# RWKV-7 rounds of a hybrid diffusion backbone: another order, another substitution and another sharing of copies

## The reference, cut to what matters

```python
def rwkv7_scan(r, w, k, v, a, b, state):
    def step(S, inp):
        r_t, w_t, k_t, v_t, a_t, b_t = inp
        sa = jnp.einsum('bhvk,bhk->bhv', S, a_t)
        S = S * w_t[:, :, None, :] + sa[..., None] * b_t[:, :, None, :] + v_t[..., None] * k_t[:, :, None, :]
        return S, jnp.einsum('bhvk,bhk->bhv', S, r_t)
```

## Time and profile before

| what | us |
|---|---|
| median of three runs | 2333.25 (2330.16 to 2334.47) |
| span of the profiled execution, first to last instruction | 2316.3 |
| PE busy / PEld busy / DVE busy / ACT busy / POOL busy | 1964.1 / 1364.9 / 941.6 / 702.3 / 330.4 |
| the RWKV rounds (`rwkv_chunks`), from the first z product to the last addition to y | 1426.4 to 1846.8, 420.4 |
| of these: round 0 (front only), until the first X product | 20.6 |
| rounds 1 to 8 | 399.8 |

### The profile page before, as it was taken

How to read it: one execution, slowest core, us unless ns; L and a number is a source line. 1 busy time by engine, 2 the same in 40 slices (tenths; PEclk the granted TensorE clock), 3 DMA queues, 4 the chain that set the end, 5 groups by cost and what they waited for, 6 DMA issues and landing times. The chain is left out here.

```text
span 2316.3 us, 58391 instructions
## 1 busy us (share of the span) xinstructions
PE 1964.1 (85%) x26021; PEld 1364.9 (59%) x26021; DVE 941.6 (41%) x1675; ACT 702.3 (30%) x1525; POOL 330.4 (14%) x211
## 2 busy tenths in 40 slices
PE   6999998997979888998487895888888897977775
PEld 3777765445844445555253685888878755633443
DVE  3183235785051111111434577666777453111112
ACT  3234534674230000100214344455444212000001
POOL 1433310002401000000110345212311000000000
PEclk8999999998989989999799997999999977988888
DMA  8554533204265789777530220000000025899975
GB/s 298 189 204 146 183 144 146 74 1 145 73 258 217 280 302 349 277 272 285 212 111 1 70 77 28 4 5 5 4 4 4 31 91 206 301 387 365 358 295 182
DMA packets 133329, 381.14 MB, mean 165 GB/s; under 512 B 14394, under 2 KB 43670, under 8 KB 115926
## 3 DMA queue, kind: packets, MB, share of 16 engines
q1 hardware_dynamic: 114528, 343.82, 40.3%
q10 hardware_dynamic: 15094, 20.99, 3.0%
q0 software_dynamic: 3456, 12.58, 1.4%
HBM read 634.54 MB, written 25.95 MB: 285 GB/s over the span
## 5 line engine op out<-in xcount | busy, mean ns | idle before, releaser
L371 PE MATMUL banks<-parts 128*128 128x512 f32 (+1 forms) x1096 | 244.7, 375 | 14.5 <-POOL parts L1523 7.6
L1814 PE MATMUL banks<-arena 128*32 128x256 f32 x1696 | 218.4, 403 | 40.8 <-DMA arena<-in_exp_w_up_dram 40.8
L371 PEld LDWEIGHTS banks<-parts 128*128 128x128 f32 x1096 | 194.6, 192 | 55.2 <-POOL parts L2388 9.4
L1815 PE MATMUL banks<-arena 128*32 128x256 f32 x1696 | 218.3, 402 | 0.0
L2561 PE MATMUL banks<-arena 64*64 64x64 f32 x4224 | 159.4, 225 | 47.7 <-DVE arena L382 18.5
L1880 ACT ACTIVATE arena<-banks 64x256 f32<-64x256 f32 x78 | 29.6, 380 | 549.9 <-PE banks L1815 382.6
L2561 PEld LDWEIGHTS banks<-arena 64*64 64x64 f32 x4224 | 147.7, 140 | 52.3 <-DVE arena L382 19.9
L1814 PEld LDWEIGHTS banks<-arena 128*32 128x32 f32 x1696 | 102.0, 115 | 120.5 <-DMA arena<-in_exp_w_up_dram 44.0
L371 PE MATMUL banks<-arena,ring 128*128 128x256 f32 (+2 forms) x560 | 163.3, 459 | 9.4 <-PEq L318 8.5
L2561 PE MATMUL banks<-ring 64*64 64x64 f32 x4224 | 159.9, 225 | 8.6 <-issue 7.4
L379 DVE TENSOR_TENSOR arena<-banks,arena 64x256 f32<-64x256 f32 (+3 forms) x128 | 65.5, 511 | 241.5 <-ACT arena L1880 149.9
(11 more groups left out here) (373 smaller groups left out, 3626.8 us busy)
## 6 DMA issues: line engine op xcount, KB each, us to landing
arena<-in_exp_w_gate_dram SPq DMA_DIRECT2D x106, 1024.0 KB
arena<-in_exp_w_up_dram SPq DMA_DIRECT2D x106, 1024.0 KB
arena<-in_exp_w_down_dram SPq DMA_DIRECT2D x53, 2048.0 KB
ring<-in_exp_w_gate_dram SPq DMA_DIRECT2D x50, 1024.0 KB
ring<-in_exp_w_up_dram SPq DMA_DIRECT2D x50, 1024.0 KB
ring<-in_exp_w_down_dram SPq DMA_DIRECT2D x25, 2048.0 KB
ring<-in_w_mod_dram SPq DMA_DIRECT2D x24, 2048.0 KB, 8.9
ring<-in_ab_w_in_dram SPq DMA_DIRECT2D x10, 2048.0 KB, 13.9
```

The costliest lines, as they stand in the source:

```text
L371: m = nc.tensor.matmul(o, a, b, start=first and n == 0, stop=last and n == len(pairs) - 1)
L1814: nc.tensor.matmul(o[r:r + BLOCK, 0:256], x, up[:, k, c], start=k == 0, stop=k == KD - 1)
L1815: m = nc.tensor.matmul(o[64 + r:64 + r + BLOCK, 0:256], x, gate[:, k, c], start=k == 0, stop=k == KD - 1)
```

## The change

Layout and names: `natural` gets D4, D4t, K4t, T2, N, KN, Nt and V1, so that D4, D4t, T2, T4, D8t, N, Nt, N2, V1 and V2 run on all four tiles (`both`); D2, D2t, T8 and U remain on two (`each`). The wide products are gone; each result has a bank of its own.

Inverse: DVE (or ACT) no longer adds T2 and T4; instead K2t = D2t + 1 and K4t = D4t + 1 are formed from PSUM, and the products are T2 = K2t T1, T4 = K4t T2; only T8 is a sum with T4. Substitution: N, its transpose Nt (one more product), KN = N + 1 and N2 = Nt N; then V1 = T8 W, V2 = KN V1, U = N2 V2 + V2. Instead of three products in a row after V1 there are two, and N2 beside them.

Accumulation in PSUM: W is opened with AK vt and a S is added to it (`opening`, `adding`); Y is opened with S r and the two others are added to it. The wide product a (S b) is therefore split into a S and Xt.

Order: the products X and Xt of the next round (`pe first`, `pe second`), their masks and T1 on DVE (`dve first`, `second`, `third`), and the z product of the round after it (`pe decay`) stand in the tail of this round, among V1, N2, V2 and U.

Sharing: of T2, T4, W, V1 and V2 the copy of direction 0 is ACT's and that of direction 1 is DVE's. The halves of the sigmoids are folded into constants (kk is halved, a is scaled by -2, ka_half), so that the ACT pass after the gate's tanh goes; POOL now makes t from the tanh, DVE makes (A + 1) Pinv, POOL makes b from it. Pinc is computed only for latent chunks, the end of the decay directly by ACT.

Lines taken away are left out below where the function is printed above.

```diff
+            s.update(b=s["A"], k=s["t"], T1=s["T"], T2=s["T"], T4=s["T"], T8=s["T"], K2t=s["W"])
+            s.update(D4=s["D"], D4t=s["Dt"], K4t=s["D2"], D8t=s["D2t"], N=s["D"], KN=s["Dt"], Nt=s["D2"], N2=s["Ot"],
+                     V1=s["D2t"], V2=s["D2"], U=s["D2"])
...
+        natural = ("a", "b", "k", "r", "S", "Y", "z", "za", "D4", "D4t", "K4t", "T2", "N", "KN", "Nt", "V1")
...
+            def head(n_, a, b, d, p, hf, start, stop):
+                rows = half(d, hf, a)
+                assert rows == half(d, hf, b)
+                return nc.tensor.matmul(view(d, n_)[half(d, hf, n_), p, :], now[d][a][rows, p, :], now[d][b][rows, p, :], start=start, stop=stop)
+            def both(n_, *pairs):
+                for p in range(8):
+                    for q, (a, b) in enumerate(pairs):
+                        for d, hf in four:
+                            m = head(n_, a, b, d, p, hf, q == 0, q == len(pairs) - 1)
+                m.then_inc(pe_done, pe.tick((n, n_ + " product", 0), (n, n_ + " product", 1)))
+            def opening(n_, a, b):
+                for p in range(8):
+                    for d, hf in four:
+                        m = head(n_, a, b, d, p, hf, p == 0, False)
+                m.then_inc(pe_done, pe.tick((n, n_ + " opened")))
+            def adding(n_, *pairs):
+                pe.wait_ge(*at_((n_ + " opened",)))
+                for p in range(8):
+                    for q, (a, b) in enumerate(pairs):
+                        for d, hf in four:
+                            m = head(n_, a, b, d, p, hf, False, p == 7 and q == len(pairs) - 1)
+                m.then_inc(pe_done, pe.tick((n, n_ + " product", 0), (n, n_ + " product", 1)))
+            def each(n_, a, b, d):
+                for p in range(8):
+                    for hf in range(2):
+                        m = head(n_, a, b, d, p, hf, True, True)
+                m.then_inc(pe_done, pe.tick((n, n_ + " product", d)))
...
+            def pe_decay():
+                take("z")
+                low_rank("z", b_w2, b_tw)
+            def pe_first():
+                take("X", "D")
+                for d in range(2):
+                    from_last(d, "a", "b")
+                both("X", ("b", "a"))
+            def pe_second():
+                take("Xt", "Ot")
+                both("Xt", ("a", "b"))
             def pe_round():
+                following = rounds[n + 1] if front else None
+                if not main:
+                    pe_decay()
                 if main:
+                    take("AK")
                     for d in range(2):
+                        from_last(d, "k")
+                    both("AK", ("k", "a"))
+                    if seg == 1:
+                        take("RK")
+                        for d in range(2):
+                            from_last(d, "r")
+                        both("RK", ("k", "r"))
+                    take("D2")
                     for d in range(2):
+                        ready(d, "D", "Dt")
+                        each("D2", "Dt", "D", d)
+                    take("D2t", "D2t", "K2t")
+                    for d in range(2):
+                        each("D2t", "D", "Dt", d)
+                    if seg == 1:
+                        take("RB")
+                        both("RB", ("b", "r"))
+                    take("D4")
+                    for d in range(2):
+                        ready(d, "D2", "D2t")
+                    both("D4", ("D2t", "D2"))
+                    take("D4t", "D4t", "K4t")
+                    both("D4t", ("D2", "D2t"))
+                    take("T2")
+                    for d in range(2):
+                        ready(d, "K2t", "T1")
+                    both("T2", ("K2t", "T1"))
+                    take("bt")
                     turned("bt", [s["b"] for s in st])
+                    take("kt")
                     turned("kt", [s["k"] for s in st])
                 if front:
+                    take("za")
                     low_rank("za", b_a2, b_al)
                 if main:
+                    take("D8t")
                     for d in range(2):
+                        ready(d, "D4", "D4t")
+                    both("D8t", ("D4", "D4t"))
+                    take("T4")
                     for d in range(2):
+                        ready(d, "K4t", "T2")
+                    both("T4", ("K4t", "T2"))
+                    take("vt")
+                    turned("vt", [chunk(b_v, seg, i, d) for d in range(2)])
+                    take("T8")
                     for d in range(2):
+                        ready(d, "D8t", "T4")
+                        each("T8", "D8t", "T4", d)
+                    take("W")
                     for d in range(2):
+                        ready(d, "AK", "vt")
+                    opening("W", "AK", "vt")
+                    take("N", "N", "KN")
+                    for d in range(2):
+                        ready(d, "T8", "Ot")
+                    both("N", ("Ot", "T8"))
+                    for d in range(2):
+                        from_last(d, "S")
+                    adding("W", ("a", "S"))
+                    take("Nt")
+                    both("Nt", ("T8", "Ot"))
+                    take("V1")
+                    for d in range(2):
+                        ready(d, "W")
+                    both("V1", ("T8", "W"))
+                if front:
+                    following["pe first"]()
+                if main:
+                    take("N2")
+                    for d in range(2):
+                        ready(d, "N", "Nt")
+                    both("N2", ("Nt", "N"))
+                    take("V2")
+                    for d in range(2):
+                        ready(d, "KN", "V1")
+                    both("V2", ("KN", "V1"))
+                if front:
+                    following["pe second"]()
                 if seg == 1:
+                    take("Y")
+                    opening("Y", "S", "r")
+                if main:
+                    take("U")
                     for d in range(2):
+                        ready(d, "N2", "V2")
+                        each("U", "N2", "V2", d)
+                    if front and following["front"]:
+                        following["pe decay"]()
                     for d in range(2):
+                        ready(d, "U", "bt", "kt", "RB", "RK")
+                    if seg == 1:
+                        adding("Y", ("U", "RB"), ("vt", "RK"))
+                    take("S")
+                    both("S", ("bt", "U"), ("kt", "vt"))
+                elif following["front"]:
+                    following["pe decay"]()
...
+                    if next_seg == 1:
+                        act.wait_ge(*at_(("next end", d)))
+                        fn(d, "Pinc", s["Pinc"], s["G"], ACT.Exp, scale=-LWC)
                 if front:
                     for d in range(2):
...
+                        squashed("z", d, "sw", 0)
+                        act.wait_ge(*at_(("tanh z", d)))
+                        fn(d, "sw", now[d]["sw"], now[d]["sw"], scale=0.5, bias=0.5)
                 if main:
+                    copied("D2")
+                    copied("D2t")
                     for d in range(2):
...
+                        act.wait_ge(*at_(("T1", d)))
+                    copied("D4")
+                    copied("D4t")
+                    copied("T2", (0,))
                 if front:
                     decays(0)
+                    decays(1)
                 if main:
+                    copied("bt")
+                    copied("kt")
+                if front:
                     for d in range(2):
...
+                        squashed("za", d, "A", 1)
                 if main:
...
+                    copied("D8t")
+                    copied("T4", (0,))
+                    copied("vt")
+                    copied("N")
+                    copied("W", (0,))
+                    copied("Nt")
+                    copied("V1", (0,))
+                    copied("N2")
+                    copied("V2", (0,))
...
+            def dve_first():
+                for d in range(2):
+                    dve.wait_ge(*at_last(("N2 product", d)))
+                    masked("D", "X", d, 2, "D read")
+            def dve_second():
+                for d in range(2):
+                    dve.wait_ge(*at_last(("V2 product", d)))
+                    masked("Dt", "Xt", d, 4)
+                for d in range(2):
+                    go(vadd(now[d]["T1"], now[d]["D"], one_of_heads), d, "T1")
+            def dve_third():
+                for d in range(2):
+                    dve.wait_ge(*at_last(("U product", d)))
+                    masked("Ot", "Xt", d, 5, "Ot read")
             def dve_round():
                 v = nc.vector
+                following = rounds[n + 1] if front else None
                 def scan_decay(d):
                     s = now[d]
```

(51 more changed lines are left out.)

352 lines of the change are left out of this document (59 added, 293 removed).

## The result

| | median, us | runs |
|---|---|---|
| before | 2331.70 | 2319.51 to 2334.47 |
| after | 2370.78 | 2366.27 to 2376.01 |

The ratio of the two is 1.0181 (95% interval 1.0151 to 1.0212): the change costs some 42 us, 1.8% (the medians above differ by 39). A later series on another chip gave 1.0187 (1.0146 to 1.0229). The forecast was slower by 16.8 us with a range of 2324 to 2375: the median lies inside the range and the direction holds, but the size is two and a half times the forecast.

What follows compares the result with a forecast made beforehand. PE bound by instruction supply, 3.66 us per two products: 1451.2 + 408.1 - 1.8 (first block) + 3 (waits) + 3.1 (end) = 1863.6 against 1846.8, so +16.8 us, median 2350, range 2324 to 2375.

Steps and rivals of the forecast that it cites:

- step 1: RWKV rounds on PE: 28 more products, 14 more instruction packets, +51 us of supply, whatever the tiles.
- Rival (a): RWKV rounds: starving is a local mishap and four-tile products run at 0.93 us; median 2243, 9%.
- step 4: Round 0 and its end: X can start at about 1444.9 instead of 1447.0; AK waits for k until 1451.2.
- The period: Instruction packet for two products: mean 3.66 us of 3.47 and 3.84, which would give 2329 and 2370.
- step 3: PE waits in the rounds: 1.79 us a block free for DVE or ACT waits; -35 us, leaving about 3.
- Rival (c): Round tails: DVE and POOL become the bound as b and k come late, 3 us a round; 2374, 12%.
- Rival (d): TensorE gets the lower clock because it is busy less, some 70 us more in two-tile halves; 2420, 2%.
- The median: Whole kernel: span 2316.3 us against run median 2333.25, so 17 us around the span, taken as unchanged.

Runs made afterwards that it cites:

- bare stretches: Kernel before plus 24-product stretches without waits, output unaffected: 3.59 us a pair on four tiles, 3.73 on two, 3.58 with 128 columns on four.
- e10: Changed kernel with TensorE's waits gathered, one per semaphore at its highest value: ratio to before 1.0122, stage 446.7 us.
- e3: Changed kernel with VectorE's (A + 1) Pinv moved ahead of the sums T8, so b comes earlier: ratio to before 1.0163, stage 453.0 us.
- e12: Changed kernel with both TensorE's waits gathered and (A + 1) Pinv moved ahead of the sums T8: ratio to before 1.0096, stage 444.7 us.
- bare blocks: Kernel before plus product pairs with VectorE waits at shifted places: 3.72 us per 128 passes with one wait; separate semaphore instruction 5.21 early, 3.70 late.

## Why the prediction was right in direction and short in size

**The bound and the count (step 1): right.** The stage has 14592 passes and 114 packets against 100; the page 219 against 205. Two products take about the same time on two tiles and on four (3.73 and 3.59 in the bare stretches, +2.5 us for the whole kernel on two tiles). "issue" is 115 us, DVE's 2.4 us waits are gone.

**Rival (a), tiles: refuted** by the bare stretch (3.59 where it gives 1.87). By the Trainium skill (Runtime: NRT & Kernel Launch, Instruction fetch mechanics) the crossing of a block is mostly hidden; with 128 passes of 64 columns in a block it is not, here ("issue" 115 us) or in the bare block (PE idle for 42% of it).

**Round 0 (step 4): right.** X starts 18.7 us after z (forecast 18.5), the first AK 24.9 (forecast 24.8).

**The period: a little short.** The mean of two rows, 3.66, against 3.74 in the intervals without a long wait. Times 111 that is 9 us. It was the term called uncertain, and the error is inside its bounds. That the upper bound (3.84, 2370) lands on the measured median is luck: the period wasn't 3.84.

**Waits (step 3): the step that failed.** Its rule, that each block has 1.79 us in which a wait for DVE or ACT is free, is true for a wait that stands with the matmul: 80 waits of 1.60 us took as long as 80 of 0.87, and 0.2 us a pair more than none. It is false for a wait in a semaphore instruction of its own among the first 37 loads of a block, behind which the next packet comes only 1.0 us after the wait's end: 5.21 instead of 3.70 us, 1.5 more for a wait of 1.15. (That the packet's request is what is held back is my reading; the trace shows the packet, not the request.) The change brings 195 such instructions instead of 116 and, by the new order, eight waits at such places, behind which stand 11 us of long intervals (before has at least one, at 1695.9). Price: 12 to 13 us by the long intervals that go in e10, 16 to 19 by its stage. The waits themselves were foreseen (b up to 0.5 us late was forecast, 1.66 was measured: that too was mis-sized; e3, with A Pinv ahead of T8's sums, has none of it), and step 3 left 3 us in all where the long intervals hold 14.4.

Together: in the stage the forecast was 437.2 us (1863.6 less 1426.4), measured 462.6. Period 9, long intervals 14, remaining 2. e10, without the separate waits, has 446.7, which is the forecast and the period's 9. e10 saved 4 to 6 us more than its long intervals hold; 2 of them are the half packet, the rest is not settled.

**Rival (c), POOL late: named the right place with the wrong price.** POOL is named before X as it said, but the waits of 1.66 us are under its threshold of 1.8, and with the waits gathered the stage is within 2 us the same with them and without (e10, e12). It is no bound: "issue" is 115 us, which it had small. That its time, 2374, is near the 2370.78 measured is luck.

**Rival (d), clock: not seen**; 0.96 in the rounds, 0.97 before. Its price was also summed too low: five products in four rounds and six in four, 1.9 us each, are 84 us, not 70.

**The median.** That 17 us lie around the span was a wrong reading: in after's runs the time is 1.8 us above the span (2373.49 and 2371.7), so the execution profiled before was one of about 2318 us, and the other 15 are how far it lay from the median. The forecast of the difference doesn't depend on it.

## What to carry to other kernels

Count TensorE's instructions when its matmuls are small: here a packet of 256 lasts 3.5 to 4 us, so 128 passes that take less than that on the tiles are bound by supply, and more tiles don't help; fewer products, or more columns in each, can, where nothing else is waited for instead (12 products fewer left the time of before as it was). Where the supply binds, a wait carried by the matmul was nearly free (1.6 us in each packet, for 0.2), so wait once for each semaphore at its highest value and let the last signal be the one on the matmul. Before calling a wait hidden, look in the trace in which form it stands and whether the next packet comes at its usual distance.

## What the runs showed of the hardware that was not expected

- A semaphore instruction of TensorE's queue on which it stands within the first 37 loads of a block delays the next packet of q8 until about 1.0 us after the wait's end (0.96 to 1.17 in after); at 46 loads and behind it doesn't. The same wait with the matmul delayed it in the bare blocks at no place by more than 0.6 us.
- In the steady part of the bare stretches, 128-column products took 3.58 us a pair against 3.59 with 64 columns and as many instructions: twice the columns in the same time.
- Two tiles took 3.73 us a pair, their own time (2 x 1.87), four tiles 3.59: the packets came at little more than the pace of two tiles.
